# Second block: the short-range heads' jobs go first, two of their scores stand among the latent units, and the selection is added inside the attention

## The reference, cut to what matters

```
h = x * (1 + scale) + shift
p_cq, p_ckv, p_kr, p_qb, p_kb, p_vb, p_qc, p_kc, p_vc, p_qi, p_ki, p_wi, p_gate = split(h @ w_in)
qa = rms_norm(p_cq) @ w_uq          # 6 latent heads: 64 plain + 32 turned features each
ka = rms_norm(p_ckv) @ w_uk; va = rms_norm(p_ckv) @ w_uv
o_a = causal softmax attention of the 6 latent heads, with rotary part
o_b = 6 short-range (dilated) heads: causal, ALiBi slope, log-count of three windows
o_c = 4 sparse heads: only the top 64 keys of an index score sum_h w * relu(q_idx . k_idx)
y = concat(o_a, o_b, o_c) * silu(p_gate)
x = layer_norm(ALPHA * x + (1 + gate) * (y @ w_out))
```

## Time and profile before

| | us |
|---|---|
| median of 3 runs | 1389.36 |
| profiled execution | 1389.1 |
| its span | 1387.3 |
| TensorE busy | 1327.9 |
| DVE busy | 991.2 |
| ScalarE busy | 670.5 |
| GpSimd busy | 192.8 |
| attention, layer 1 (1122.0 to 1154.3), TensorE busy | 28.39 |
| attention, layer 2 (1318.0 to 1352.0), TensorE busy | 29.81 |

### The profile page before, as it was taken

How to read it: one execution, slowest core, us unless ns; L and a number is a source line. 1 busy time by engine, 2 the same in 40 slices (tenths; PEclk the granted TensorE clock), 3 DMA queues, 4 the chain that set the end, 5 groups by cost and what they waited for, 6 DMA issues and landing times. The chain is left out here.

```text
span 1387.3 us, 24593 instructions
## 1 busy us (share of the span) xinstructions
PE 1327.9 (96%) x9158; PEld 1161.7 (84%) x9158; DVE 991.2 (71%) x1722; ACT 670.5 (48%) x1348; POOL 192.8 (14%) x274
## 2 busy tenths in 40 slices
PE   7999998999999999989999899999999998899987
PEld 6786776888888888878896899999899978899967
DVE  6798786899887877976339565565665985765974
ACT  4437743531624316343238564466455565465663
POOL 0101212000000000212006600000220016020034
PEclk9999998999999999989999999999999999899989
DMA  8782133467985858825220345765374533355601
GB/s 319 262 247 91 53 116 122 152 212 227 306 300 206 303 201 294 282 70 149 86 92 1 113 143 161 206 184 179 125 265 154 181 108 116 127 178 166 197 32 47
DMA packets 67657, 234.85 MB, mean 169 GB/s; under 512 B 7280, under 2 KB 12400, under 8 KB 67312
## 3 DMA queue, kind: packets, MB, share of 16 engines
q1 hardware_dynamic: 67568, 233.67, 51.8%
HBM read 232.59 MB, written 1.05 MB: 168 GB/s over the span
## 5 line engine op out<-in xcount | busy, mean ns | idle before, releaser
L849 DVE TENSOR_TENSOR wlo<-raw,whi 128x1024 fp32r<-128x1024 f32 x284 | 349.9, 1233 | 172.1 <-ACT whi L551 165.0
L551 ACT ACTIVATE whi<-raw 128x1024 fp32r<-128x1024 f32 x284 | 299.4, 1055 | 246.6 <-PE ps L1475 244.0
L1473 PE MATMUL ps<-Hh,whi 128*128 128x512 f32 (+1 forms) x848 | 297.7, 351 | 10.2 <-DVE Hl L985 8.3
L1474 PE MATMUL ps<-Hl,whi 128*128 128x512 f32 (+1 forms) x848 | 294.5, 347 | 0.0
L1475 PE MATMUL ps<-Hh,wlo 128*128 128x512 f32 (+1 forms) x848 | 294.2, 347 | 0.0
L1473 PEld LDWEIGHTS ps<-Hh,whi 128*128 128x128 f32 x848 | 162.4, 191 | 35.9 <-issue 11.8
L1473 PE MATMUL ps<-Gh,whi 128*128 128x256 f32 x624 | 178.1, 285 | 3.8 <-DVE Gl L985 3.8
L1475 PEld LDWEIGHTS ps<-Hh,wlo 128*128 128x128 f32 x848 | 162.3, 191 | 21.5
L1474 PEld LDWEIGHTS ps<-Hl,whi 128*128 128x128 f32 x848 | 162.4, 191 | 20.6
L1474 PE MATMUL ps<-Gl,whi 128*128 128x256 f32 x624 | 176.9, 284 | 0.0
L1475 PE MATMUL ps<-Gh,wlo 128*128 128x256 f32 x624 | 176.8, 283 | 0.0
(11 more groups left out here) (232 smaller groups left out, 2043.0 us busy)
## 6 DMA issues: line engine op xcount, KB each, us to landing
raw<-wall SPq DMA_DIRECT2D x284, 512.0 KB, 4.3
aring<-aall SPq DMA_DIRECT2D x144, 512.0 KB, 4.7
AL<-ali SPq DMA_DIRECT2D x14, 192.0 KB, 5.3
X<-xin SPq DMA_DIRECT2D x2, 1024.0 KB, 6.4
BI<-rpb SPq DMA_DIRECT2D x4, 512.0 KB, 10.0
out<-X SPq DMA_DIRECT2D x4, 256.0 KB, 2.3
cst<-const SPq DMA_DIRECT2D x1, 960.0 KB, 8.5
par<-prm SPq DMA_DIRECT2D x1, 134.5 KB, 2.1
```

The source lines that it names most:

```text
L551: act.activation(whi[:, slot, :], raw[:, slot, :], ACT.Copy).then_inc(sem("w_hi"), 1)
L849: dve.tensor_tensor(wlo[:, slot, :], raw[:, slot, :], whi[:, slot, :].bitcast(F32), ALU.subtract)\
L1473: pe.matmul(o, a[0], b[0], start=first, stop=False)
L1474: pe.matmul(o, a[0], b[1], start=False, stop=False)
```

## The change

Four things, in both layers. (1) The jobs' order is short-range (0 to 2), latent (3 to 5), sparse (6, 7), and the output projection contracts its row tiles in the order 3, 4, 5, 0, 1, 2, 6, 7. (2) The latent units (`p_uq` with `high=True`, keys, values) write banks 4 to 7, and their turned tiles use `wk2` and `MO` instead of `wk1`. (3) The scores of jobs 0 and 1 stand after the second of the five latent query units on TensorE; their maxima stand on DVE after `ahead` of the third and of the fourth (`steps(.., 0, 3)`, maxima, `steps(.., 3, 4)`, maxima, `steps(.., 4, 5)`); their exponentials on ScalarE after the evacuation of the third and the fourth. TensorE's transposes of job 0 wait for VA. (4) The selection is computed in place in `IX` and added to `AL` by DVE inside `attend`, before the maxima of job 3, and no longer before the attention.

```diff
+            def bank(self, i):
+                return (self.o0 + i) % 4 + (4 if self.high else 0)
+            def turned(self, r):
+                return wk2[:, 2 + r % 2, :] if self.high else wk1[:, r % 2, :]
+            def swapped(self, r):
+                return MO[:, r % 2, :] if self.high else wk1[:, 2 + r % 2, 0:N]
...
+        B2_ORDER = (3, 4, 5, 0, 1, 2, 6, 7)
...
# ScalarE
                 for i in range(5):
                     ahead(u0 + 37 + i)
                     evac(p_uq[l], i)
+                    if i in (2, 3):
+                        exps(J_B2[l][0] + i - 2)
                 ahead(u0 + 42)
                 act.wait_ge(sem("w_used"), u0 + 43)
                 for i in range(3):
-                    act.activation(KN[:, i, :], ps[:, (p_uk[l] + i) % 4, 0:N], ACT.Copy).then_inc(sem("proj_out"), 1)
+                    act.activation(KN[:, i, :], ps[:, 4 + (p_uk[l] + i) % 4, 0:N], ACT.Copy).then_inc(sem("proj_out"), 1)
                 ahead(u0 + 43)
                 evac_v(u0 + 43, V_UV[l], [VA[:, t, :] for t in range(2)])
-                act.wait_ge(sem("sb_done"), l + 1)
-                attend(*J_B2[l])
+                attend(*J_B2[l], begun=2)
...
# DVE
+            def attend(j0, j1, begun=0, select=None):
                 for s in range(j0, j1 + 4):
+                    if select is not None and s == j0 + 3:
+                        dve.tensor_scalar(IX[:, :], IX[:, :], -2.0e38, NEG, ALU.is_gt, ALU.mult).then_inc(sem("sel_done"), 1)
+                        dve.wait_ge(sem("sel_done"), select + 1)
+                        dve.tensor_tensor(AL[:, 6:10, :], AL[:, 6:10, :], IX[:, None, :].to_broadcast([P, 4, 384]), ALU.add)\
+                           .then_inc(sem("sb_done"), 1)
+                        dve.wait_ge(sem("sb_done"), select + 1)
                     if j0 + begun <= s < j1:
                         maxima(s)
...
-                if p == TOPK // 8 - 1:
-                    dve.tensor_scalar(SEL, IX[:, :], -2.0e38, NEG, ALU.is_gt, ALU.mult).then_inc(sem("sel_done"), 1)
...
-                steps(p_uq[l], 0, 5)
+                dve.wait_ge(sem("ali_landed"), 16 * (10 + 4 * l))
+                steps(p_uq[l], 0, 3)
+                maxima(J_B2[l][0])
+                steps(p_uq[l], 3, 4)
+                maxima(J_B2[l][0] + 1)
+                steps(p_uq[l], 4, 5)
                 ahead(u0 + 42)
                 ahead(u0 + 43)
-                dve.wait_ge(sem("ali_landed"), 16 * (10 + 4 * l))
-                dve.wait_ge(sem("sel_done"), l + 1)
-                dve.tensor_tensor(AL[:, 6:10, :], AL[:, 6:10, :], SEL[:, None, :].to_broadcast([P, 4, 384]), ALU.add)\
-                   .then_inc(sem("sb_done"), 1)
-                dve.wait_ge(sem("sb_done"), l + 1)
-                attend(*J_B2[l])
+                attend(*J_B2[l], begun=2, select=l)
...
# TensorE
-                pe.wait_ge(sem("nlo"), norms[f"q{l}"].h0 + 6)
-                project(p_uq[l], 0, 5, Cx, kts=6)
                 pe.wait_ge(sem("nlo"), norms[f"kv{l}"].h0 + 2)
+                project(p_uq[l], 0, 2, Cx, kts=6)
+                pe.wait_ge(sem("proj_out"), p_uq[l].o0)
+                scores(J_B2[l][0])
+                scores(J_B2[l][0] + 1)
+                project(p_uq[l], 2, 5, Cx, kts=6)
...
-                pe.wait_ge(sem("proj_out"), V_UV[l] + 2)
                 pe.wait_ge(sem("rope_out"), p_uq[l].r0 + 2)
-                attend(*J_B2[l])
-                project_out(u0 + 44, 16 + 8 * l, 256, Gx, ("o_lo", [HL[J_B2[l][0] + k] for k in range(KT)]))
+                attend(*J_B2[l], begun=2, values_out=V_UV[l] + 2)
+                project_out(u0 + 44, 16 + 8 * l, 256, Gx, ("o_lo", [HL[J_B2[l][0] + n] for n in range(KT)]), order=B2_ORDER)
```

More of the change, by code:

```diff
@@ L282, in program, with __init__ @@
             ropes = 0
-            def __init__(self, u0, tiles):
+            def __init__(self, u0, tiles, high=False):
                 self.u0, self.tiles = u0, tiles
+                self.high = high
                 self.o0, self.r0 = Proj.outs, Proj.ropes
@@ L347, in program @@
                                       Tile(256, "h", QR[0:64, 1, :], None, 96 ** -0.5)]
-                             + [Tile(256, None, QN[:, i, :], None, 96 ** -0.5) for i in range(3)]))
+                             + [Tile(256, None, QN[:, i, :], None, 96 ** -0.5) for i in range(3)], True))
             p_uk.append(Proj.outs)
@@ L412, in program @@
                 jobs.append(Job(
+                    q=(lambda p, r, i=i: QZ[rows(r), i, P * p:P * p + P]),
+                    k=(lambda p, r, i=i: KQ[rows(r), i, 0:KLEN[p]]), parts=KLEN,
+                    bias=AL[:, 2 * i:2 * i + 2, :],
+                    v=(lambda p, kt, r, i=i: V2[:, kt, N + 64 * (2 * i + r):N + 64 * (2 * i + r) + 64]),
+                    dst=(Gh[:, 3 + i, :], Gl[:, 3 + i, :]), gate=GT[:, 3 + i, :]))
+            for i in range(3):
+                jobs.append(Job(
                     q=(lambda p, r, i=i: QN[rows(r), i, P * p:P * p + P]),
@@ L419, in program @@
                     dst=(Gh[:, i, :], Gl[:, i, :]), gate=GT[:, i, :]))
[L420 to L426, removed]
             for i in range(2):
@@ L599, in evac @@
                 act.wait_ge(sem("w_used"), pr.u0 + i + 1)
-                bank = ps[:, o % 4, :]
+                bank = ps[:, pr.bank(i), :]
                 if t.rope is None:
@@ L607, in evac @@
                     act.wait_ge(sem("rope_out"), r - 1)
-                ins = act.activation(wk1[lo:hi, r % 2, 0:N], bank[lo:hi, 0:N], ACT.Copy, scale=t.scale)
+                ins = act.activation(pr.turned(r)[lo:hi, 0:N], bank[lo:hi, 0:N], ACT.Copy, scale=t.scale)
                 if t.rest is not None:
@@ L1025, in rope @@
                     dve.wait_ge(sem("rope_out"), r - 1)
[L1026 to L1027 removed]
+                turned, swapped = pr.turned(r)[lo:hi, :], pr.swapped(r)[lo:hi, :]
+                link(dve.stream_shuffle(swapped, turned[:, 0:N], SWAP))
                 link(dve.tensor_tensor(swapped, swapped, cst[lo:hi, sines:sines + N], ALU.mult))
                 dve.wait_ge(sem("rope_cos"), r + 1)
[L1030 removed]
+                dve.tensor_tensor(t.dst, turned[:, N:2 * N], swapped, ALU.add).then_inc(sem("rope_out"), 1)
             def steps(pr, lo, hi):
@@ L1585, in project @@
                             T = pr.tiles[i].T
-                            ins = mm3(ps[:, (pr.o0 + i) % 4, 0:T], wtile((pr.u0 + i) % SLOTS, P * k, P),
+                            ins = mm3(ps[:, pr.bank(i), 0:T], wtile((pr.u0 + i) % SLOTS, P * k, P),
                                       (x[0](k)[:, 0:T], x[1](k)[:, 0:T]), k == 0, k == kts - 1)
@@ L1685, in sub_turn, with project_out @@
                   .then_inc(sem("sub_tr"), 1)
-            def project_out(u0, o0, T, x, ready, late={}):
+            def project_out(u0, o0, T, x, ready, late={}, order=range(KT)):
                 name, counts = ready
@@ L1695, in project_out @@
                             pe.wait_ge(sem("out_added"), o0 + i - 3)
-                    for k in range(KT):
+                    for n, k in enumerate(order):
                         if group[0] == 0:
-                            if k in late:
-                                sub_turn(late[k])
-                            pe.wait_ge(sem(name), counts[k])
+                            if n in late:
+                                sub_turn(late[n])
+                            pe.wait_ge(sem(name), counts[n])
                         for i in group:
                             ins = mm3(ps[:, i % 4, 0:T], wtile((u0 + i) % SLOTS, P * k, P),
-                                      (x[0](k)[:, 0:T], x[1](k)[:, 0:T]), k == 0, k == KT - 1)
-                            if k == KT - 1:
+                                      (x[0](k)[:, 0:T], x[1](k)[:, 0:T]), n == 0, n == KT - 1)
+                            if n == KT - 1:
                                 ins.then_inc(sem("w_used"), 1)
```

11 lines of the change are left out of this document (5 added, 6 removed).

## The result

The changed kernel took 1395.13 us (median of 6 runs, 1393.08 to 1396.22), the kernel before beside it 1389.44 us (1387.23 to 1390.73): ratio 1.0033, 95% interval 1.0021 to 1.0044. It is slower by 5.7 us by the medians, by 2.9 to 6.1 us by the ratio's interval; 6.0 were forecast, as were the sign and the range. Its profiled execution took 1393.09 us, with a span of 1391.2.

What follows compares the result with a forecast made beforehand. TensorE, busy 96% of 1387.3 us, was taken as the bound. Losses of 2.8 to 4.1 us in the first layer and 1.9 to 3.2 in the second, together 4.7 to 7.3, middle 6.0, gave 1395.4 us; range 1388.5 to 1400.5.

Steps and rivals of the forecast that it cites:

- Steps 1 to 6: Latent units: early scores make ScalarE stand twice, and TensorE 5.2 us before the values' unit, until 1125.6.
- ring of waits: Latent units: ScalarE waits for early maxima, DVE's low part of u0+43 for a high part queued behind job 0's exponentials.
- Step 7: TensorE, after the values' unit: first transposes at 1129.3, only 1.1 us ahead of the kernel before.
- Step 8: DVE in the attention: selection and addition, 2.4 us, lose their cover; job 4's maxima start at 1137.0, level with before.
- Step 9: Late attention: job 5's latent score, 2.11 us, delays its maxima to 1141.2; first layer +1.3 us at full clock.
- The clock term: After TensorE's stand: low clock until 1130.7 to 1134.8 costs the first layer 1.5 us, or 2.8 if job 3's score is slow.
- Two of its signs: First latent unit to output projection grows from 48.9 to 52 to 53 us; nothing before 1105 moves.
- The third rival, "the clock stays up": Attention of both layers without a fall of the clock: +1.3 and +0.4, in sum +1.7 us, 1391.1; chance 0.17.
- The fourth: Fifth latent evacuation doesn't hold the values' unit; transposes start at 1123.1, -5.5 us a layer, 1378 us; chance 0.08.

Runs made afterwards that it cites:

- clock held up: Changed kernel with 36 idle TensorE products in its stand before the latent values' unit: 1390.04 us, beside 1390.34 for the kernel before, ratio 1.0002.
- repeat: The changed kernel measured again, unedited: 1393.19 us against 1389.79 for the kernel before, ratio 1.0020.
- kernels of 1401.57 us: Changed kernel with scores, maxima and exponentials of jobs 0 and 1 put back behind the latent units: median 1391.21 us, slowest run 1401.57.
- 1391.17 us: Changed kernel with later exponentials and early maxima of jobs 0 and 1, and the selection moved into a VectorE gap: median 1390.19 us.

## Why the prediction was right, step by step

Times of its steps are taken from the first latent unit (1105.40 in before, 1107.16 after), so that what lies ahead of it drops out.

*Steps 1 to 6 held.* Early scores 1.58 us (1.8 forecast); ScalarE's stands 2.89 and 2.95 (2.7 and 3.0); VectorE's idle time before the low part 2.73 (2.8); TensorE's stand 5.00 (5.2), the values' unit 20.46 after the first latent unit (20.2). The experiment on job 1's maxima shows the ring of waits as the cause: with the maxima ahead of the low part, 3 us of the stand go.

*Step 7 held at full clock*: first transposes 23.9 us after the first latent unit, both as forecast and in the changed kernel with the clock held up. With the fall of the clock they came at 25.5, so the start that was to be early was 0.5 us later than in before (25.02).

*Step 8 was priced right, but its price is hardly on the path.* Selection and addition took 2.2 us between the maxima of jobs 2 and 3 (2.4 forecast). Job 4's maxima came 31.4 us after the first latent unit with the clock held up (31.6 forecast). The forecast had this on the path through VectorE, which taken alone would be 2.1 us a layer; moving both instructions away brought 0.3. TensorE's own scores and transposes take about as long, so VectorE only waits for them instead (1.39 us before job 4's maxima). That the two paths are level is what the forecast didn't see.

*Step 9 held.* Job 5's maxima wait 1.03 us for their score, and start at 35.7 us with the clock held up (1142.60 less 1106.94; 35.8 forecast). The layer then ends 1.1 us after before's first and 0.2 us after its second (1.3 and 0.4 forecast).

*The clock term was somewhat too large.* Forecast were 1.5 or 2.8 us a layer. Against the 50.0 us with the clock held up, the profiles of the changed kernel and its repeat show 0.8 to 1.2; those with the selection's instruction moved or written elsewhere, which have the same stand, 1.9 and 2.0 in their first layers and 1.1 in their second. The forecast let the low clock start when TensorE resumes and last 5.1 to 9.2 us from there. In these eight layers the low stretch was 6.9 to 7.0 us long, but it began 1.0 to 3.9 us before TensorE resumed, so that part of it passed while TensorE stood anyway, and 3.0 to 5.9 us were left: below the forecast's 5.1 in six layers, within it in two, and never enough for the 2.8. The kernel before had shown this already: in its second layer the clock was low from 1323.1, 1.3 us before TensorE resumed (read in steps of 0.1 us, as the stretches here), which the row that starts at 1323.60 leaves out. With 1.0 in place of 1.5 to 2.8 the same sum gives 1.3 + 0.4 + 2.0 = 3.7 us, near the 3.6 of the profiles and the 3.4 of the repeat.

*So the 6.0 beside the measured 5.7 is in part luck.* Sign and causes were right, and a loss of 2.9 to 6.1 us is what the first measurement allows. But of the profiles with the stand of 5.0 us none shows more than 4.4 us in the two stretches together (52.00 and 51.10 us, with the selection written elsewhere), and the repeat's medians give 3.4; both are below the 4.7 at which the forecast's sum began. Two of its signs failed as well: the first stretch grew to 51.1 and not to 52 to 53 us, and the first latent unit, ahead of which nothing was to move, came 1.8 us later. The two profiles of the changed kernel, which differ there by 1.3 us, make that a matter of the run more than of the edit.

*The third rival, "the clock stays up", was +1.7 us*; with the clock held up the ratio was 1.0002 (0.9992 to 1.0012), and the two layers 1.3 us longer than in before's profile. The fourth decided where it was said to: with the fifth evacuation out of the exponentials' way the transposes came at 19.7 us (17.7 forecast, its 1123.1), and with the clock held up the layers took 3.6 and 4.5 us less than in the kernel before, not 5.5. That kernel moves both early maxima, both early exponentials and the selection together, so what each brings there isn't shown.

*What the sum hid.* It set a new schedule, at full clock, against an old profile with 2 to 3 us of low clock within. For the total that is right, but the +1.3 a layer looks like the price of the schedule, and is not. Clock for clock the change loses 3.1 us a layer (50.0 against 46.9), 6.2 in both: the early scores, as placed, cost 3.6, and order, banks and selection together gain 0.5 (46.4 against 46.9). Order and banks were not taken apart. The low clock takes 2.1 and 2.9 us from the kernel before and only 1 to 2 from the changed one, and hides the rest.

## What to carry to other kernels

Before work is moved forward between two engines, write out both queues behind every new wait: a wait whose release needs something queued behind another wait of the same pair costs twice, and here one job's maxima, put ahead of one low part, turned a loss of 3 to 6 us into a gain of 4.3. A stand of TensorE is priced twice as well, as its own length and as the chance that what follows runs at half speed; if a kernel's runs spread over 15 us, hold the clock up with idle products in the stand and compare then. A gain that is measured against a profile with a low clock in it must be set against the same kernel at full clock.

## What the runs showed of the hardware

*What the low clock costs varies from run to run, and goes with what follows the stand.* The clock fell around a stand of 1.69 us in one layer and stayed up in the other of the same execution. Where the 384-column products of the values' unit followed, it was back 3.0 to 6.3 us after TensorE resumed (13 falls, in the changed kernel and those in which only VectorE's order or the selection's output differ); where scores of 64 rows and transposes followed, it came 8.0 and 9.1 us after in before and over 24 us after in the kernels of 1401.57 us (both layers) and 1391.17 us (one), though TensorE was busy without a gap. That the kind of product decides was not tested by itself. The Trainium skill (TensorE: Matmul & The Clock Gate, "What's actually happening") calls the number of slow products at a kernel's start run-variable; these falls lie in the middle of a kernel, and the spread of 1383 to 1402 us for one kernel shows the same of them.

*VectorE's instruction waits for GpSimd beside it.* 128x384, one tensor input: 0.35 us alone, 0.70 us where GpSimd's product of two buffers had 0.48 or 0.49 us left to run, in place or not, and 0.48 us at the same place in the program where it had 0.27 us left. In all six rows of this kind VectorE's ends 0.21 or 0.22 us after GpSimd's. So it is held until GpSimd is done, or nearly, and not run at half pace; that it came to twice the time is chance. A GpSimd copy of 0.40 us that overlapped it by 0.11 us left it at 0.35. The Trainium skill (VectorE: DVE Perf Modes, "Mode 2×_2P — use both read ports for one tensor") says that such an instruction reads its one input through both ports; the runs show the wait, not the port.
